# A two-layer retrieval decoder: second weight table for 96 tokens, scalar-form VectorE operations in the first half of the down stage, and a finer-grained head

## The reference, cut to what matters

```
q = (ht @ w_q).reshape(T, 8, 2, 128)                  # 8 heads, two halves
s1, s2 = q[:, :, 0] @ k1.T, q[:, :, 1] @ k2.T         # 128 keys each
top 16 of each, top 16 of their 256 sums -> sc, idx = e1 * 128 + e2
gate = softmax(sc)
act = gelu(x . u_tab[idx])                            # "up"
out = sum of gate * act * v_tab[idx]                  # "down"
```

## Time and profile before

| | |
|---|---|
| Runs | 1806.35, 1812.38, 1812.19 us; median 1812.19 |
| Profiled execution | 1807.06 us, of which the span of the profile is 1805.4 |
| Mean granted TensorE clock | 0.992 of full speed |
| PE / PE weight load / DVE / ACT / POOL busy | 98% / 88% / 80% / 51% / 47% of the span |
| First down stage, in span time | 576.1 to about 930 us; its middle near 755 |
| Second down stage | 1436.5 to about 1790 us; its middle near 1616 |

### The profile page before, as it was taken

One profiled execution on the slowest core, in us unless ns is written; L12 is line 12 of the kernel. 1 busy time (PEld: TensorE's weight loads), 2 busy tenths in 40 slices (PEclk: granted clock), 3 DMA queues, 4 the chain that ended last, 5 costly groups with the idle time before them and its releaser, 6 DMA issues.

```text
span 1805.4 us, 34572 instructions
## 1 busy us (share of the span) xinstructions
PE 1765.9 (98%) x11751; PEld 1593.7 (88%) x11751; DVE 1443.1 (80%) x2758; ACT 928.3 (51%) x1449; POOL 839.8 (47%) x489
## 2 busy tenths in 40 slices
PE   6999999999999999999998999999999999999998
PEld 6988999999888888888888899999988888888887
DVE  8998789997777966698888778999787796666665
ACT  3345555555555445454555546556555554545453
POOL 1000066777877888510000005677777888841000
PEclk9999999999999999999999999999999999999998
DMA  8998889867766988999945756777777698886662
GB/s 322 325 338 315 273 256 303 252 175 189 175 172 166 249 233 242 295 362 334 325 164 179 265 164 164 186 179 183 186 175 179 164 244 234 241 262 205 209 207 85
DMA packets 191697, 414.23 MB, mean 229 GB/s; under 512 B 77696, under 2 KB 95488, under 8 KB 190976
## 3 DMA queue, kind: packets, MB, share of 16 engines
q1 hardware_dynamic: 126768, 405.36, 66.7%
q0 software_dynamic: 62976, 5.49, 8.6%
q10 hardware_dynamic: 1872, 2.39, 0.4%
HBM read 387.60 MB, written 25.54 MB: 229 GB/s over the span
## 4 chain that ended last, share of the span: by engine, by line
PE 93%; DVE 5%; issue 1%; DMA 1%; ACT 1%; SPq 0%; DVEq 0%; ACTq 0%
PE acc L1779 38%; PE ps L1597 31%; PE ps L1614 7%; PE acc L1614 5%; PE ps L1617 4%; PE acc L1617 2%; PE gp L1729 2%; DVE acts L857 2%; PE ps L1571 1%; DVE low L833 1%; PE gp L1718 1%; DMA acts<-w_mod 1%; DVE acts L924 0%; PE gp L1533 0%; DVE mov L956 0%
## 5 line engine op out<-in xcount | busy, mean ns | idle before, releaser
L833 DVE TENSOR_TENSOR low<-raw,high 128x1024 fp32r<-128x1024 f32 x596 | 724.0, 1217 | 276.1 <-ACT high L546 273.5
L546 ACT ACTIVATE high<-raw 128x1024 fp32r<-128x1024 f32 (+1 forms) x593 | 624.7, 1054 | 375.3 <-PE acc L1779 300.8
L494 POOL DMA_INDIRECT table<-added x256 | 466.3, 1821 | 585.4 <-DVE added L1080 452.7
L1779 PE MATMUL acc<-high,mov 128*128 128x512 f32 x2048 | 633.9, 390 | 2.7 <-DVE mov L1382 2.7
L1597 PE MATMUL ps<-mov,high 128*128 128x256 f32 x3280 | 594.0, 284 | 7.2 <-issue 2.7
L1597 PEld LDWEIGHTS ps<-mov,high 128*128 128x128 f32 x3280 | 511.0, 192 | 9.1 <-issue 6.1
L1597 PE MATMUL ps<-mov,low 128*128 128x256 f32 x1640 | 463.9, 283 | 0.0
L1779 PEld LDWEIGHTS acc<-high,mov 128*128 128x128 f32 x2048 | 384.4, 188 | 84.4 <-DVE mov L1382 2.7
L1779 PE MATMUL acc<-low,mov 128*128 128x512 f32 x1024 | 398.4, 389 | 0.0
L1597 PEld LDWEIGHTS ps<-mov,low 128*128 128x128 f32 x1640 | 314.6, 192 | 0.0
L1779 PEld LDWEIGHTS acc<-low,mov 128*128 128x128 f32 x1024 | 192.2, 188 | 39.6
(11 more groups left out here) (156 smaller groups left out, 1410.8 us busy)
## 6 DMA issues: line engine op xcount, KB each, us to landing
raw<-up SPq DMA_DIRECT2D x256, 512.0 KB
raw<-down SPq DMA_DIRECT2D x256, 512.0 KB
acts<-w_mod SPq DMA_DIRECT2D x84, 512.0 KB, 5.8
raw<-query SPq DMA_DIRECT2D x32, 512.0 KB
table<-hot SPq DMA_DIRECT2D x32, 512.0 KB, 6.7
raw<-conv_in SPq DMA_DIRECT2D x24, 512.0 KB
mov<-table SPq DMA_DIRECT2D x96, 128.0 KB, 4.3
acts<-w_mod SPq DMA_DIRECT2D x6, 1024.0 KB, 14.9
```

Source lines behind the costliest of these rows:

```text
L494: nc.gpsimd.indirect_dma_start(table[layer], bass.IndirectOffsetOnAxis(ap=DEST[:, col:col + 1], axis=0), GT0[:, col:col + 1], None, comput ...
L546: nc.scalar.activation(taken_of(n, flat(high[s])), taken_of(n, tile_row(s)), ACT.Copy).then_inc(high_ready, 1)
L833: nc.vector.tensor_tensor(taken_of(n, flat(low[n % RING])), taken_of(n, tile_row(n % RING)), w, ALU.subtract).then_inc(low_ready, 1)
L1779: ins = nc.tensor.matmul(acc[:, b, :], w[:, s, tok], flat(v[s])[:, cols], start=(opening and n == 0), stop=(closing and n == 2), skip_grou ...
```

## The change

It has three parts.

1. `LATE_T` goes from 80 to 96 and `LATE_UP` from 112 to 116. `LATE_SETS` becomes 12, the second table has six groups of 16 adds per layer, 96 in all, and four one-hot sets per layer are left for the second half of the experts, where there were six. The late fetches and multiplications get 192 elements per partition instead of 160.
2. In the first half of the down stage `rest_of`, `low_weight` and `weigh_first` are issued as `scalar_tensor_tensor` with the factor 1.0 in place of `tensor_tensor` (function `two`). The results are the same.
3. In the head the 16 blocks are 16 transfers; DVE makes the sum of the scale after the fourth shift block, does the last shift block in two halves of 512 columns, and the shift is summed by PE and taken by DVE in two halves. The orders of DVE, ACT and PE around it change, and PE has fewer matmuls on zeros.

```diff
@@ -32,8 +32,8 @@
 SET = 8
 SETS = P // SET
 PAIRS = SET // 2
-LATE_T = 80
-LATE_UP = 112
+LATE_T = 96
+LATE_UP = 116
 LATE_SETS = LATE_T // SET
...
 
-HEAD = [(1, 0, 1), (1, 1, 1), (1, 2, 2), (1, 4, 2), (1, 6, 2), (0, 0, 2), (0, 2, 2), (0, 4, 2), (0, 6, 1), (0, 7, 1)]
+HEAD = [(m, k) for m in (1, 0) for k in range(DC)]
...
         macc_done = sem("macc_done")
...
 
-            for n, (m, k, ks) in enumerate(HEAD):
+            for n, (m, k) in enumerate(HEAD):
                 if n == 2:
                     sp.dma_start(A[:, 0:DC * T], x_in).then_inc(x_in_s, 16)
                 if n == len(HEAD) - 2:
                     load(0, "conv_in", 0, 0)
-                sp.dma_start(mhead[:, m, k:k + ks],
-                             w_mod[0, k * P:(k + ks) * P, m * D:(m + 1) * D].rearrange("(k p) n -> p k n", p=P)
...
+                def first_tile(n):
+                    arrived(1, n)
+                    nc.scalar.activation(flat(high[n]), tile_row(n), ACT.Copy).then_inc(high_ready, 1)
+
                 if k == 0:
-                    for n in range(AHEAD):
-                        arrived(1, n)
-                        nc.scalar.activation(flat(high[n]), tile_row(n), ACT.Copy).then_inc(high_ready, 1)
+                    for n in range(2):
+                        first_tile(n)
                 shift = mod[:, (3 * (k % 2)) * DC:(3 * (k % 2) + 1) * DC]
 
-                act.wait_ge(mod_taken, 4 * (2, 4, 6, 6)[k])
+                act.wait_ge(mod_taken, 6 if k == 0 else 4 * (2, 4, 6, 6)[k])
                 for c in range(DC):
+                    if k == 0 and c == DC // 2:
+                        act.wait_ge(mod_taken, 8)
                     act.wait_ge(xr_done, DC * k + c + 1)
                     nc.scalar.activation(mov_h[:, c], xr[:, c], ACT.Identity,
                                          bias=shift[:, c:c + 1]).then_inc(mh_done, 1)
+                if k == 0:
+                    first_tile(2)
...
@@ -825,17 +832,23 @@
             def turn(v, n):
                 return v.rearrange("p (r n) -> p r n", n=n)
 
-            def rest_of(n):
+            def two(out, a, b, op, beside_pool=False):
+
+                if beside_pool:
+                    return nc.vector.scalar_tensor_tensor(out, a, 1.0, b, ALU.mult, op)
+                return nc.vector.tensor_tensor(out, a, b, op)
+
+            def rest_of(n, beside_pool=False):
 
                 if n < TILES:
                     dve.wait_ge(high_ready, n + 1)
                     w = taken_of(n, flat(high[n % RING])).bitcast(F32)
-                    nc.vector.tensor_tensor(taken_of(n, flat(low[n % RING])), taken_of(n, tile_row(n % RING)),
-                                            w, ALU.subtract).then_inc(low_ready, 1)
-
-            def slot(n):
-
-                rest_of(n + AHEAD)
+                    two(taken_of(n, flat(low[n % RING])), taken_of(n, tile_row(n % RING)), w, ALU.subtract,
+                        beside_pool).then_inc(low_ready, 1)
+
...
-            def head_mod(m):
-
-                for n, (block_, k0, ks) in enumerate(HEAD):
-                    if block_ == m:
-                        dve.wait_ge(mhead_in[n], 16)
-                        for k in range(k0, k0 + ks):
-                            link(add_mod(m, mhead[:, m, k], k, k == 0))
-                dve.sem_inc(macc_done, 1)
+            def head_block(m, k, n0=0, n1=D):
+
+                dve.wait_ge(mhead_in[HEAD.index((m, k))], 16)
+                v, c, to = mhead[:, m, k, n0:n1], cact[:, k:k + 1], macc[:, m, n0:n1]
+                if k == 0:
+                    return nc.vector.tensor_scalar(to, v, c, None, ALU.mult)
+                return nc.vector.scalar_tensor_tensor(to, v, c, to, ALU.mult, ALU.add)
+
+            def finish_shift(c0, c1):
+
+                dve.wait_ge(shift_half, c0 // (DC // 2) + 1)
+                nc.vector.tensor_tensor(mod[:, c0:c1], acc[:, c0 // (DC // 2), c0:c1],
+                                        sm[:, C_BM + c0:C_BM + c1], ALU.add).then_inc(mod_taken, 2)
...
-                dve.wait_ge(msum_done, sums[0])
+                dve.wait_ge(msum_done, sums[0] - (sums[0] > 2))
...
-            def norm(k, shift_last=None):
...
                 if k == 0:
-                    head_mod(1)
+                    for n in range(DC - 1):
+                        link(head_block(1, n))
+                    head_block(1, DC - 1).then_inc(macc_done, 1)
...
                 if k == 0:
-                    head_mod(0)
-                    link(nc.vector.memset(vp[:, :, 0:TAPS - 1], 0.0))
+                    for n in range(4):
+                        link(head_block(0, n))
                     finish_mod(0, 1, 2)
...
-                for c in range(DC):
-                    if k == 0 and c == 2:
-                        rest_of(0)
-                        shift_last()
-                    scaled(c)
                 if k == 0:
+                    for n in range(4, DC - 1):
+                        link(head_block(0, n))
+                    for h in range(2):
+                        head_block(0, DC - 1, h * D // 2, (h + 1) * D // 2).then_inc(macc_done, 1)
+                    scaled(0)
+                    scaled(1)
+                    finish_shift(0, DC // 2)
+                    scaled(2)
+                    scaled(3)
+                    finish_shift(DC // 2, DC)
+                    sums[0] += 1
+                    scaled(4)
+                    scaled(5)
+                    rest_of(0)
+                    scaled(6)
+                    scaled(7)
                     rest_of(1)
-                if k == 2:
-                    rest_of(AT[1, "pool_in"] + 2)
-                if k < 4:
+                    dve.wait_ge(mod_taken, 8)
                     for c in range(DC):
                         rest(c)
-                if k == 0:
+                    link(nc.vector.memset(vp[:, :, 0:TAPS - 1], 0.0))
                     rest_of(2)
+                else:
+                    for c in range(DC):
+                        scaled(c)
+                    if k == 2:
+                        rest_of(AT[1, "pool_in"] + 2)
+                    if k < 4:
+                        for c in range(DC):
+                            rest(c)
...
                 nc.vector.tensor_tensor(a, a, g, ALU.mult).then_inc(weighted, 1)
 
-            def weigh_first(layer, q):
+            def weigh_first(layer, q, beside_pool=False):
 
                 dve.wait_ge(wt_in[q % WRING], 16 * (layer * (GROUPS // WRING) + q // WRING + 1))
                 a = A[:, WTILES * q * T:WTILES * (q + 1) * T].rearrange("p (g t) -> p g t", t=T)[:, :, 0:P]
-                nc.vector.tensor_tensor(a, a, wt[q % WRING].rearrange("p (g t) -> p g t", t=P),
-                                        ALU.mult).then_inc(weighed, 1)
+                two(a, a, wt[q % WRING].rearrange("p (g t) -> p g t", t=P), ALU.mult, beside_pool
+                    ).then_inc(weighed, 1)
 
...
                 quarters(5)
 
-                def low_weight(g):
+                def low_weight(g, beside_pool=False):
                     if g < KEYS:
                         s = g % RING
                         dve.wait_ge(wh_ready, g + (layer * KEYS + 1))
-                        nc.vector.tensor_tensor(mov_l[:, s], A[:, g * T:(g + 1) * T], mov_h[:, s].bitcast(F32),
-                                                ALU.subtract).then_inc(wl_ready, 1)
+                        two(mov_l[:, s], A[:, g * T:(g + 1) * T], mov_h[:, s].bitcast(F32), ALU.subtract,
+                            beside_pool).then_inc(wl_ready, 1)
 
...
                 for j in range(HALF):
-                    slot(n0 + j)
+                    slot(n0 + j, True)
                     if j + AHEAD < HALF:
-                        low_weight(j + AHEAD)
+                        low_weight(j + AHEAD, True)
                     if j < 7:
                         if j % 2 == 0:
-                            weigh_first(layer, j // 2 + 2)
+                            weigh_first(layer, j // 2 + 2, True)
                     else:
-                        weigh_first(layer, j - 1)
+                        weigh_first(layer, j - 1, True)
                     if j % 8 == (2 if j >= 8 else 3) and j // 8 * 2 < SETS - LATE_SETS:
                         two_sets(1, j // 8 * 2 + LATE_SETS)
...
-            def mod_products(m, c0=0, c1=DC):
+            def sum_scale():
+
+                sums[0] += 1
+                for c in range(DC):
+                    ins = nc.tensor.matmul(gp[:, 1, DC + c:DC + c + 1], macc[:, 1, c * P:(c + 1) * P],
+                                           ones[:, 0:1], start=True, stop=True)
+                ins.then_inc(msum_done, 1)
+
+            def sum_shift(c0, c1):
 
                 for c in range(c0, c1):
-                    ins = nc.tensor.matmul(gp[:, 1, m * DC + c:m * DC + c + 1], macc[:, m, c * P:(c + 1) * P],
+                    ins = nc.tensor.matmul(acc[:, c0 // (DC // 2), c:c + 1], macc[:, 0, c * P:(c + 1) * P],
```

(54 more changed lines are left out.)

2 lines of the change are left out of this document (added).

## The result

The changed kernel takes **1866.3 us** (median of 4, 1865.29 to 1872.79) where the kernel before took 1811.65 beside it (1806.35 to 1812.38): ratio 1.030, 95% interval 1.026 to 1.034. The forecast of 1808.9, its range of 1800 to 1820 and its 0.71 for "the same" were wrong; what happened is rival A, which had 0.15. The profiled execution took 1866.48 (span 1864.6), 59.2 us of span more than before's.

A forecast was written before the change was run, and what follows sets the result against it. TensorE was taken as the bound, with 93% of the chain. -2.94 - 1.0 + 0.6 = -3.3 us took the profiled 1807.06 to 1803.8; with the median 5.1 higher the forecast was 1808.9 us, range 1800 to 1820.

The forecast's parts named there:

- rival A: Down stage's first half: scalar form holds POOL like the plain one; PE waits 38.6 and 32.5 us, 1880 us; chance 0.15.
- Step 3: Late adds beside scalar-form operations: 1.90 us each with issue, so they end at 737.5, 5 us before the date.
- the pair at 434.36: Add and wide scalar-form operation started together; the add's 1.55 us was taken as a sign of no hold.
- the upper mechanism: Late adds: scalar form holds POOL back as the plain form does, 2.72 us per add.
- Step 2: POOL's 16 more adds per layer must end by 742.8: 1.96 us each in the first layer, 2.06 in the second.
- Steps 1 and 6: Second half of experts: one scatter pair less per layer, 2.94 us saved; head: tail gain 1.0 us (0.6 to 1.3).
- Step 4: Scalar form's price on DVE: 60 ns per operation, 0.15 us per layer at the middle; together +0.6 us.
- Rival C: Scalar form on DVE runs at half rate, 3.5 us per tile against 2.72: 1900 us; chance 0.01.
- Step 5: Shelf read at tile 116: 11.1 of 12.2 us used, so no cost; bound 2 us per layer; wider fetches also free.

The follow-up runs named there:

- e1: Kernel after with plain two-tensor operations put back in the first half of the down stage: 1869.05 us, ratio 1.033 to the kernel before.
- e4: Kernel after with the first-half low-part subtraction of the down stage replaced by a one-source maximum (those low parts not computed): 1802.3 us, ratio 0.995.
- e5: Kernel after with the first-half low-part subtraction of the down stage in two plain halves of 512 columns: 1823.14 us, ratio 1.003.
- e8: Kernel before (80 tokens, old head) with the first-half low-part subtraction of the down stage in two halves of 512 columns: 1806.28 us, ratio 0.996.
- e2: Kernel after with the second table back at 80 tokens and shelf read at tile 112, scalar form and new head kept: 1814.94 us, ratio 1.002.
- e7: Kernel before with the new head alone (80 tokens, plain form): 1813.69 us, ratio 1.000.
- e3: Kernel after with the sixth group of adds left out, 80 of 96 per layer, table still 96: 1816.25 us, ratio 1.002.
- e6: Kernel after with the first-half low-part subtraction of the down stage in four plain quarters of 256 columns: 1833.16 us, ratio 1.011.
- e10: Kernel before with DVE waiting for its own low-part subtraction's end, once per tile of the down stage's first half: 1808.03 us, ratio 0.997.

## Why the prediction was wrong

**Step 3 failed.** "The form with a scalar" was given the lower bound, 1.90 us per add, on the pair at 434.36. The runs show the upper mechanism: 2.42 us beside it, as beside the plain form, 2.60 per add with the issue, and e1 gives the same time without it. The reasoning was weak where it said it was: the add and the operation began in the same 10 ns. The trace of before had plain operations with the same start, and the adds passed them too, while one that began 0.02 us later was held:

```profile
582.33 0.99 DVE L1221 TENSOR_TENSOR hot<-hot,gate 128x1536 bf16<-128x1536 bf16 x1
582.33 1.55 POOL L505 DMA_INDIRECT late<-gate  x1 [0.30 <-issue]
...
1442.73 0.95 DVE L1221 TENSOR_TENSOR hot<-hot,gate 128x1536 bf16<-128x1536 bf16 x1
1442.75 2.36 POOL L505 DMA_INDIRECT late<-idx  x1 [0.30 <-issue]
```

Twelve late adds of before began in the same 10 ns as a plain operation with two sources in SBUF, five of them with the low-part subtraction itself, and each took 1.55 or 1.56 us. So the pair at 434.36 could not tell the forms apart. Against it stood 44 adds, most of them held by an operation that reads the same two SBUF operands. By the Trainium skill, SBUF — State Buffer, section Who interferes with whom, a Vector instruction with two SBUF inputs contends with a GpSimd instruction that reads SBUF, and one with at most one SBUF input does not, outside DVE's two-port modes. The runs agree with both halves (1866 and 1869 us for the kernel after and e1, 1802 for e4, and the 22 adds beside `weigh`).

**Rival A** named the place and the mechanism, and the price roughly: waits of 38.6 and 32.5 us, measured 28.4 and 32.2. The first was 10 us too long, mainly for two of its terms. From the last add's end to the first weighting it put 8.4 us, and it was 778.70 - 774.26 = 4.4, with the DMA engines busy for 0.25 of that time, where it was 0.92 in before from 742.7 to 746.8; and 14 adds, not 11, had begun by 576, some 5 us. In the second layer the first helps as well, but the adds began at 1436.30, nearly 4 us later than before's 1403.68 moved by the 28.8 us that the layer starts later: the two cancel, so the close figure of 32.5 is in part luck. The 2.4 us of clock behind each gap it did not have.

**Step 2 was right that 80 adds are just in time, but its bound of 1.96 us is not one.** It rests on the 8.4 us from the last add's end to the first weighting, read from one execution, and on a date at 751.2. Both move. The way took 4.4 us in the kernel after and 13.0 in e5 (746.28 to 759.25), and without a wait e5's DVE would have started the weighting at 759.25 - 12.58 = 746.67. So e5's adds end 3.5 us behind the 742.8 of step 2 and DVE waits 12.6; with e5's own distances step 2's formula gives (746.67 - 13.0 - 576)/85 = 1.86. e4, with 1.86 per add (1.56 + 0.30), ends at 735.6 and doesn't wait. Even adds at 1.96 would have been late beside e5's landing. The profiled execution of before waited 0.94 us, and I took this for the rule, while most runs are slower than it; that the 5 us between its time and the median, which the forecast carried along, are missed dates is likely by the table at e8, not shown.

**Steps 1 and 6 fit.** e4 (96 tokens, new head, no wait) against e8 (80, old head, no wait): 1802.3 and 1806.3, 4.0 us less for the 2.94 + 1.0 forecast. The two ran on different chips, so the norms' marks are the better measure: the stretch of the first layer's experts is 793.7 in e4 and 795.9 in e8, the last stretch 799.2 and 800.7, 3.7 us for two pairs. In before and e2, which have no wait of PE for the adds either, these stretches are 795.5 and 796.7, then 802.9 and 802.4, so the figure is good to 2 or 3 us only. The head's share is 0.7 (e7), also with an uncertainty of some tenths.

**Step 4 was mis-sized:** it took 60 ns per operation from groups whose scalar is read from SBUF. With the constant 1.0 there is next to nothing:

```profile
L838 DVE SCALAR_TENSOR_TENSOR low<-raw,high 128x1024 fp32r<-128x1024 f32 x128 | 156.7, 1224 | 86.4 <-ACT high L546 85.7
```

1224 against 1217 ns, and PE's wait at the middle is 0.66 us in e2 and 0.68 in e4, against 0.66 before, where the forecast added 0.15. Rival C falls with the same row.

**Step 5 was right:** PE has no gap at tile 116 in the kernel after (busy 25.96 of the 26 us from 526 to 552), and e3 carries the whole of that step without a price that shows.

## What to carry to other kernels

An engine off the critical path with a date needs its slack measured over many executions, not in one: a kernel whose times spread by 1% may be missing a date most of the time, and here the gain was to let that work end sooner (e8), not to load it further. Where DVE must run beside GpSimd's indirect adds, ask how many of its operands come from SBUF; another opcode with the same operands changed nothing. Cutting the operation shortened the hold where DVE had pauses left. And a pair of rows that begin in the same 10 ns is no evidence of what either does to the other.

## What was not expected of the hardware

- An operation with two sources in SBUF held an add for the rest of its own length in the steady part (0.87 us), but in a stretch without pauses one add was held across ten operations (6.2 us more in e3) or longer (18.26 us in all, e6). In e4 such an add took 4.45 us and was let go at 591.88 + 4.45 - 1.54 = 594.79, where the first one-source operation began (594.82). The same is true of all 17 late adds of over 3 us in the thirteen profiled executions: each was let go within 0.25 us ahead of the first pause of DVE, or of its first operation with at most one source in SBUF, that came after the add began. Why the boundary behind a subtraction lets an add go in the steady part and not in the full one stays open.
- Two executions with the same place of the add to 10 ns went both ways (1.78 and 7.74 us). In all, 15 late adds began 0.26 to 0.33 us into the 1024-wide one-hot operation: ten were held for 4.45 to 18.26 us, and five passed at 1.78 to 1.83, one each in before, the kernel after, e1, e2 and e10.
- From the last add's end to the fetch it took 2.1 us in the kernel after, where PE, DVE and the weights' loads stood still, 4.1 in the kernel before, 6.7 in e3 and 7.8 in e5. Faster adds alone don't explain it: e4's, the fastest, had 3.5. What sets the time was not tested.
